# The first two output pairs of each down pass taken in step: products 1 to 3 of both, then 4 to 7 of each

## What is computed

```
h = x + jnp.concatenate([att, y], axis=-1) @ w_out
f = rmsnorm(h, norm_ffn)
h = h + (jax.nn.silu(f @ w_gate) * (f @ w_up)) @ w_down
```

## Time and profile before

| what | us |
|---|---|
| three runs before | 2960.06, 2960.75, 2969.58; median 2960.75 |
| the profiled execution: its time | 2968.66 |
| the profiled execution: its span | 2966.9 |
| products of the seven-product part | 1425.5 to 2779 of the span |
| first switch (pair 44) | 2380 to 2440 |
| second switch (pair 52) | 2560 to 2625 |

### The profile page before, as it was taken

The page is one execution under the profiler, slowest core; times in us unless marked ns, Lnnn a source line. Parts: engine busy times, 40 slices in busy tenths (PEclk is TensorE's granted clock), DMA queues, the critical chain, the costliest instruction groups (busy, mean ns, idle before and its releaser), DMA issues.

```text
span 2966.9 us, 49258 instructions
## 1 busy us (share of the span) xinstructions
PE 2775.7 (94%) x20329; PEld 2641.5 (89%) x20329; DVE 1705.3 (57%) x2517; ACT 1023.8 (35%) x1518; POOL 392.6 (13%) x166
## 2 busy tenths in 40 slices
PE   7999999999999987996899999999999999999997
PEld 7987898877777766996899999999999989999997
DVE  3321599444444446115777777777776787777423
ACT  5223211233333324223344344334334353443222
POOL 2222233211111101431000000000000000000231
PEclk9999999999999998998999999999999999999999
DMA  6322231555555546442333433433432365555521
GB/s 220 108 69 79 69 105 53 158 148 158 161 144 153 148 125 196 138 133 77 102 110 110 146 110 110 145 111 110 142 106 94 116 223 159 215 165 159 203 102 65
DMA packets 394448, 388.80 MB, mean 131 GB/s; under 512 B 25406, under 2 KB 354726, under 8 KB 391161
## 3 DMA queue, kind: packets, MB, share of 16 engines
q1 hardware_dynamic: 367112, 360.00, 38.6%
q10 hardware_dynamic: 27120, 25.77, 2.6%
HBM read 319.11 MB, written 68.00 MB: 130 GB/s over the span
## 4 chain that ended last, share of the span: by engine, by line
PE 71%; issue 15%; DVE 5%; POOL 5%; ACT 2%; DMA 1%; SPq 0%; ACTq 0%; POOLq 0%; DVEq 0%
PE PS L1335 43%; PE PS L890 16%; PE PS L1317 5%; POOL WL L782 4%; PE PS L1085 1%; PE PS L1282 1%; PE PS L1269 1%; PE PS L1056 1%; DMA xin<-in_x_sample 1%; PE PS L1113 1%; PE PS L1075 1%; POOL WL L815 0%; DVE xo_t L2463 0%; PE PS L1102 0%; PE PS L1259 0%
## 5 line engine op out<-in xcount | busy, mean ns | idle before, releaser
L1335 PE MATMUL PS<-xo_t,WH 128*128 128x288 f32 x2560 | 521.5, 298 | 21.8 <-ACT kept L1744 10.1
L890 PE MATMUL PS<-AH,WH 128*128 128x288 f32 (+1 forms) x2208 | 495.6, 307 | 19.5 <-DVE AL L1886 4.7
L890 PE MATMUL PS<-AL,WH 128*128 128x288 f32 (+1 forms) x2208 | 483.0, 301 | 0.0
L890 PE MATMUL PS<-AH,WL 128*128 128x288 f32 (+1 forms) x2208 | 481.1, 300 | 0.0
L1335 PEld LDWEIGHTS PS<-xo_t,WH 128*128 128x128 f32 x2560 | 416.7, 191 | 23.4 <-issue 23.4
L890 PEld LDWEIGHTS PS<-AH,WH 128*128 128x128 f32 (+1 forms) x2208 | 366.4, 195 | 43.0 <-issue 29.9
L1335 PE MATMUL PS<-xo_x,WH 128*128 128x288 f32 x1920 | 387.3, 296 | 14.5 <-DVE xo_x L2429 14.3
L1335 PE MATMUL PS<-xo_t,WL 128*128 128x288 f32 x1280 | 380.3, 297 | 0.0
L890 PEld LDWEIGHTS PS<-AL,WH 128*128 128x128 f32 (+1 forms) x2208 | 366.4, 194 | 0.0
L890 PEld LDWEIGHTS PS<-AH,WL 128*128 128x128 f32 (+1 forms) x2208 | 364.5, 193 | 0.0
L2315 DVE TENSOR_TENSOR WL<-WRAW,WH 128x1024 fp32r<-128x1024 f32 x200 | 244.8, 1224 | 138.5 <-ACT WH L1736 137.3
(11 more groups left out here) (370 smaller groups left out, 3615.1 us busy)
## 6 DMA issues: line engine op xcount, KB each, us to landing
WRAW<-in_w_gate SPq DMA_DIRECT2D x22, 2048.0 KB
WRAW<-in_w_up SPq DMA_DIRECT2D x22, 2048.0 KB
WRAW<-in_w_down SPq DMA_DIRECT2D x32, 1024.0 KB
WRAW<-in_w_in SPq DMA_DIRECT2D x14, 2048.0 KB, 8.3
raw<-in_w_in SPq DMA_DIRECT2D x48, 512.0 KB, 4.1
kca<-in_cache_k SPq DMA_DIRECT2D x256, 64.0 KB, 2.8
vca<-in_cache_v SPq DMA_DIRECT2D x256, 64.0 KB, 2.0
WRAW<-in_w_out SPq DMA_DIRECT2D x16, 1024.0 KB, 10.4
```

Of the source, the lines that this page charges most:

```text
L890: last = nc.tensor.matmul(G[gslot][0:width, h, 0:HALF], wt[:, half if slot is None else slot, k % 8, 0:width], act[:, k, h * HALF:(h + 1) ...
L1335: last = mm(out, wt[:, k, :], act[:, m, k, :], start=(j in (0, 1, 3) and k == 0 and wt is wh and m == 0), stop=(k == 7 and wt is wl), skip ...
```

## The change

It changes three things, around both switches.

- **The order of the products.** The first 14 products of a pass, so far the seven of pair q and then the seven of pair q+1, become (q,0), (q,1), (q,2), (q+1,0), (q+1,1), (q+1,2), then (q,3) to (q,6), then (q+1,3) to (q+1,6). ACT's `keep` of (q+1,2) moves from position 6 to position 10, behind the `cast` there, since its place is taken until (q,5) has been gathered.
- **The turning of the token operands.** Operands 0 to 6 are turned at positions -4, -3, -1, 1, 3, 5, 7 instead of -4 to 2. Operand 3 is first used at position 6.
- **The order of SP.** Only operands 0 to 2 are loaded first. Then come the weights of pair q+1, then the store of the last pair's result and the loads of partial sums, and only then operands 3 to 6.

```diff
--- before.py
+++ after.py
@@ -373,10 +373,17 @@
         G0, NL = 8, NG - 8
         TL, CL = TF + 16 * (NL - 1), CD + 8 * (NL - 1)
         FIRST = (NPAIR, NPAIR + 8)
+        COUPLE = [(0, 0), (0, 1), (0, 2), (1, 0), (1, 1), (1, 2)] + [(d, j) for d in range(2) for j in range(3, 7)]
         seq = [(q, j) for q in range(NALL) for j in range(7)]
+        for q in FIRST:
+            seq[7 * q:7 * q + 14] = [(q + d, j) for d, j in COUPLE]
+        OPERAND_AT = (-4, -3, -1, 1, 3, 5, 7)
+        keeps = {c + 1: [v] for c, v in enumerate(seq) if v[1] in (0, 2, 3)}
+        for q in FIRST:
+            keeps[7 * q + 10] = keeps.pop(7 * q + 6)
         POS = {v: c for c, v in enumerate(seq)}
         ADD = {v: n + 1 for n, v in enumerate(v for v in seq if v[1] in (1, 4, 5, 6))}
-        KEEP = {v: n + 1 for n, v in enumerate(v for v in seq if v[1] in (0, 2, 3))}
+        KEEP = {v: n + 1 for n, v in enumerate(v for c in range(1, 7 * NALL + 1) for v in keeps.get(c, ()))}
         RAW = {}
         for q, j in seq:
             for what in {0: ("difference",), 2: ("second", "fourth"), 3: ("sum",)}.get(j, ()):
@@ -717,18 +724,19 @@
                 else:
                     store_sums(q - 2)
                     next_sums(q - 2)
-                for j in range(7):
+                for j in range(3):
                     load_operand(e, j)
+                load_weights(q + 1)
                 if e == 0:
                     store_hidden(NPAIR // 2 - 1)
                     load_sums(q)
-                    load_weights(q + 1)
                     sp.wait_ge(s["h_st"], 16 * (NPAIR // 2))
                     load_sums(q + 1)
                 else:
-                    load_weights(q + 1)
                     store_sums(q - 1)
                     next_sums(q - 1)
+                for j in range(3, 7):
+                    load_operand(e, j)
                 for r in range(q + 2, q + 8):
                     load_weights(r)
                     store_sums(r - 2)
@@ -1751,12 +1759,16 @@
 
             def window(c):
 
-                q1, j1 = seq[c - 1]
-                if j1 in (0, 2, 3):
-                    keep(q1, j1, q1 % 2)
+                now = keeps.get(c, ())
+                late = [v for v in now if v != seq[c - 1]]
+                for q1, j1 in now:
+                    if (q1, j1) not in late:
+                        keep(q1, j1, q1 % 2)
                 if c + 2 < NPROD:
                     q2, j2 = seq[c + 2]
                     cast(c + 2, q2, j2, (c + 2) % 3, q2 % 2)
+                for q1, j1 in late:
+                    keep(q1, j1, q1 % 2)
             for c in range(3, 32):
                 if c >= 4:
                     hi_p(C3 + c, c % 4, c // 4)
@@ -1799,8 +1811,8 @@
 
             def turn_high(e, n):
 
-                j = n + 4
-                if 0 <= j < 7:
+                if n in OPERAND_AT:
+                    j = OPERAND_AT.index(n)
                     act.wait_ge(op_in[j], 16 * e + OP_BASE[j] + 16)
                     copy(xo[OPERANDS[j]][:, 0, :, :], x_raw[OPERANDS[j]][:, :, :]).then_inc(s["x_hi"], 1)
 
```

## The result

The changed kernel takes 2978.45 us in the median (12 runs, 2970.77 to 2986.97), the kernel before 2960.51 (12 runs, 2955.77 to 2969.87). The ratio of after to before is 1.0056 with a 95% interval of 1.0043 to 1.0068: slower by 16.6 us (12.7 to 20.1), where I had forecast 15.5. The profiled execution took 2983.18 us.

What follows compares the result with a forecast made beforehand. The prediction took PE, busy 94% of the span, as the bound. It added 7.65 us at the first switch and 7.9 at the second, 15.5 in all, to the median of 2960.75: 2976 us, range 2967 to 2985.

Steps and rivals of the forecast that it cites:

- What can be won at most: PE's time lost at both switches: 24.3 us before, forecast to become about 40.
- Position 2: PE's wait in front of position 2: 4.22 us shrinks to about 1.8, the second switch's 2.51 goes.
- Operand 3 behind the store: SP issues operand 3 late, ACT stands for it; position 4 starts at 2421.4 (before 2419.50) and 2612.85 (before 2612.11).
- Positions 6 and 9: ACT's and DVE's operand work makes PE wait 2.4 us in front of position 6 and 1.9 before 9.
- The slow products: Products partly at 1.2 instead of 2.4 GHz: 1.4 us charged for position 6 per switch; position 9 slow too, 2979.
- The weights of pair q+1: Needed at position 1 and issued before position 0; costed at nothing.
- The detour isn't felt: Rival on SP: ACT finds operand 3 loaded, position 4 isn't held; up to 4 us gained, 2957, chance 0.13.
- A jammed queue: Rival at the second switch: weights still queued, store lands after 8.9 us, operand 3 after 8.1; 2986, chance 0.13.

Runs made afterwards that it cites:

- e2: The changed kernel with operands 3, 4, 5 turned at positions 3, 4, 5 instead of 1, 3, 5: 2963.87 us, 1.0014 of the kernel before.
- e3: The changed kernel with operand 3 alone loaded ahead of the store: 2964.91 us, 1.0002 of the kernel before.
- e7: The changed kernel with operand 4 loaded before operand 3 behind the store: 2985.20 us, 1.0074 of the kernel before.
- e5: e3 with operands 4, 5, 6 turned at positions 5, 6, 7 instead of 3, 5, 7: 2959.05 us, 0.9987 of the kernel before.
- e4: The changed kernel with all seven operands loaded first, then the weights of pair q+1, then the store: 2979.83 us, 1.0061 of the kernel before.
- e1: The changed kernel with the loads of operands 3 to 6 moved ahead of the store: 2969.04 us, 1.0019 of the kernel before.

## Why the prediction was right

The forecast was 2976 us, a loss of 15.5; it is 2978.45, by the ratio 16.6. The mechanism was right; that the size agrees to about 1 us is in part luck, since a slow product more or less is 1.5 us. Its steps one by one:

- **What can be won at most.** 24.3 us lost at both switches before, 42 after; about 40 was forecast.
- **Position 2.** The wait of 4.22 became 1.76 (1.8 forecast), that of 2.51 at the second switch went. The gain is real, and it is given back two products later.
- **Operand 3 behind the store.** To compare the clock times I shift the trace of after by the difference at the last point that both share, 3.11 us at the first switch. The store was issued at 2401.37 + 3.11 = 2404.5 (2404.5 forecast), operand 3 at 2408.2 (2408.4), it had landed when ACT began at 2414.3 (2414.6), and position 4 started at 2421.1 (2421.4). At the second, shifted by 4.61 the other way, position 4 started at 2613.1 (2612.85). This step was argued from the order of the queues and four durations, and every one of them held within 0.3 us. e2, e3 and e7 show that it is the cause.
- **Positions 6 and 9.** 10.5 us from position 4 to 6 at both switches (10.2 forecast; the steps as listed add up to 11.6 and not 11.5, which gives 10.3), waits of 2.40 and 1.81 in front of 6, 1.80 and 1.79 in front of 9 (2.4 and 1.9). e3 shows that they are DVE's and ACT's own, and e5 that the place of operand 4 sets the first of them.
- **The slow products.** This is the term that was mis-sized. I charged 1.4 us for position 6 at both switches and nothing for position 9. In the trace position 6 was slow at the second switch only, and position 9 at both, 4.8 and 4.7 us. At the first switch the two errors cancel by chance, at the second they don't. Every wait followed by a slow product was the case that I took from the Trainium skill, "TensorE: Matmul & The Clock Gate", and priced at 2979. The trace agrees for 7 of the 8 waits shown above, not for the one of 2.40 at the first switch (3.3 us for its product). The other traces disagree more often: behind the same wait of 1.76 the product ran at full clock in four of them. The slow position 9 is most of what the second switch has beyond the forecast, +9.8 where I had 7.9.
- **The weights of pair q+1.** I costed them at nothing, and PE nowhere waits for them in the change. e4 shows what cover they had: without it 12 us.
- **The detour isn't felt, the rival on the other side.** It is what e3 makes, and e1 at the second switch. I had priced it at 2957 with DVE's waits left in place; e3 gave 2961 by its ratio, with three slow products behind those waits.
- **A jammed queue** didn't happen in the change; the store of the second switch landed after 3.2 us. In e1 it did: the stores took 11.1 and 11.7 us to land, and the first load of sums 12.2.

What stays open: which waits are followed by a slow product. The rows show one of 2.40 without and several of 1.8 with it, before the change one of 1.86 without, and the same wait of 1.76 with it in some kernels and without it in others. With one trace of each kernel I can't say whether it differs from execution to execution.

## What to carry to other kernels

When work is spread over more positions, ask of each queue what now stands behind a wait that used to be met already. The most expensive wait isn't the one of the data that come last, but the one that stands ahead of work which doesn't need them: moving the load of one operand won back 16 of 16.6 us, moving its copy by two positions (and the next one's by one) 12.5. An engine that idles isn't free help if it shares a port with the engine it is to relieve.

## What I had not expected of the hardware

- A 1.22 us subtraction on DVE took 5.74 and 6.15 us while POOL ran one of 5 to 7 us, though the page had shown POOL as idle there. With an input in PSUM it kept its 0.45 us.
- A load of 0.59 MB took 12.2 us to land when the weights, four loads of 1.18 MB and a store stood ahead of it, and 3.7 us alone (the next one in e1).
- After waits between 1.8 and 2.5 us the next product ran either at full clock or at 0.64 to 0.73, with no rule that these rows show; 1.5 us each, up to four times in a switch, which is as much as some of the effects looked for.
